# Odd mixing stage of a four-layer fp32 network: eight projection tiles multiplied by high and low rows in one product

## The reference, cut to what matters

```python
def odd_mixer(x, w_in, sgu_g, sgu_w, sgu_b, conv_w, w_o):
    h = x @ w_in
    u, v, g_b, g_c, z = _split(h, ODD_WIDTHS)          # five times 512 columns
    u = jax.nn.gelu(u)
    v = layer_norm(jax.nn.gelu(v).reshape(bsz, seq, G_C, HEAD_DIM), sgu_g)
    v = v.reshape(bsz, seq // CHUNK, CHUNK, G_C, HEAD_DIM)
    mix = jnp.einsum('gts,bnsgd->bntgd', jnp.tril(sgu_w), v) + jnp.swapaxes(sgu_b, 0, 1)[:, :, None]
    o_c = u * mix.reshape(bsz, seq, C_WIDTH)
    o_d = g_b * causal_dwconv(g_c * z, conv_w)
    return jnp.concatenate([o_c, o_d], axis=-1) @ w_o
```

## Time and profile before

| | us |
|---|---|
| median of 3 runs | 1352.31 (1351.74 to 1355.9) |
| the profiled execution's own time | 1356.57 |
| span of the profiled execution | 1355.3 |
| TensorE busy with matmuls in it | 1332.7 (98%) |
| VectorE (DVE) | 1011.4 (75%) |
| ScalarE (ACT) | 787.8 (58%) |
| GpSimd (POOL) | 147.2 (11%) |
| mean granted TensorE clock | 0.997 of full speed |

### The profile page before, as it was taken

How to read it: one execution, slowest core, us unless ns; L and a number is a source line. 1 busy time by engine, 2 the same in 40 slices (tenths; PEclk the granted TensorE clock), 3 DMA queues, 4 the chain that set the end, 5 groups by cost and what they waited for, 6 DMA issues and landing times. The chain is left out here.

```text
span 1355.3 us, 20736 instructions
## 1 busy us (share of the span) xinstructions
PE 1332.7 (98%) x8197; PEld 1160.7 (86%) x8197; DVE 1011.4 (75%) x1658; ACT 787.8 (58%) x1282; POOL 147.2 (11%) x131
## 2 busy tenths in 40 slices
PE   7999999999999999999999999999999999999998
PEld 7987888888898788887987888888789998888887
DVE  4845588777896787778788677776567997786766
ACT  6654266655442565653677566555557875665553
POOL 4860300000100000000000000000302224000000
PEclk9999999999999999999999999999999999999999
DMA  7722355655563556553642255655344345455551
GB/s 283 267 82 121 109 202 217 234 186 186 195 249 124 187 188 246 193 194 111 216 166 102 113 202 205 221 192 196 138 163 179 127 155 188 154 188 204 195 196 71
DMA packets 38607, 242.18 MB, mean 179 GB/s; under 512 B 4448, under 2 KB 7408, under 8 KB 11120
## 3 DMA queue, kind: packets, MB, share of 16 engines
q1 hardware_dynamic: 38512, 240.87, 48.6%
HBM read 236.89 MB, written 2.64 MB: 177 GB/s over the span
## 5 line engine op out<-in xcount | busy, mean ns | idle before, releaser
L323 DVE TENSOR_TENSOR wlo<-raw,whi 128x2048 fp32r<-128x2048 f32 (+1 forms) x179 | 402.6, 2255 | 105.1 <-ACT whi L297 103.1
L297 ACT ACTIVATE whi<-raw 128x2048 fp32r<-128x2048 f32 x195 | 370.4, 1903 | 88.8 <-PE ps L475 40.4
L412 PE MATMUL ps<-XS,whi 128*128 128x512 f32 x1392 | 331.8, 390 | 0.0
L412 PEld LDWEIGHTS ps<-XS,whi 128*128 128x128 f32 x1392 | 257.8, 188 | 52.2 <-issue 0.6
L464 PE MATMUL ps<-whi,MS 128*128 128x512 f32 x960 | 233.3, 391 | 0.0
L464 PEld LDWEIGHTS ps<-whi,MS 128*128 128x128 f32 x960 | 177.5, 188 | 35.8 <-issue 0.4
L417 PEld LDWEIGHTS ps<-XS,wlo 128*128 128x128 f32 x1392 | 178.5, 191 | 6.8
L417 PE MATMUL ps<-XS,wlo 128*128 128x256 f32 x1392 | 180.6, 283 | 0.0
L392 PE MATMUL ps<-XS,whi 128*128 128x256 f32 x672 | 167.2, 289 | 0.0
L393 PE MATMUL ps<-XS,whi 128*128 128x256 f32 x672 | 163.9, 284 | 0.0
L308 POOL TENSOR_TENSOR wlo<-raw,whi 128x512 fp32r<-128x512 f32 x90 | 123.1, 1381 | 188.6 <-ACT whi L297 98.4
(11 more groups left out here) (337 smaller groups left out, 1539.5 us busy)
## 6 DMA issues: line engine op xcount, KB each, us to landing
raw<-in_up SPq DMA_DIRECT2D x88, 1024.0 KB, 4.8
raw<-in_down SPq DMA_DIRECT2D x44, 1024.0 KB, 4.9
raw<-in_hg_t SPq DMA_DIRECT2D x16, 1024.0 KB, 4.8
raw<-in_od_t SPq DMA_DIRECT2D x8, 1024.0 KB, 5.2
raw<-in_ev_a SPq DMA_DIRECT2D x6, 1024.0 KB, 10.5
raw<-in_wa_o SPq DMA_DIRECT2D x6, 1024.0 KB, 5.0
raw<-in_hg_o SPq DMA_DIRECT2D x6, 1024.0 KB, 4.9
raw<-in_ev_o SPq DMA_DIRECT2D x4, 1024.0 KB, 5.8
```

The lines of the kernel that those rows point to most:

```text
L297: ac.activation(parts_of(m)[0][:, 0:w], raw[m % NRAW][:, 0:w], ACT.Copy).then_inc(w_hi)
L323: ve.tensor_tensor(lo[:, c], r[:, c], hi[:, c].bitcast(F32), ALU.subtract).then_inc(w_lo_v)
L412: pe.matmul(banks[i][:, 0:512], hi[:, c], XS[:, k, 0:512], start=(k == 0), stop=False)
```

## The change

All eight `ot` tiles go through `project_wide` instead of `project`. So each takes two banks, and the halves are added behind it. For u: ACT copies two low halves to `U` (`u_half`), DVE adds (`u_sum`), and ACT applies gelu in place (`u_gate`). For g_c and z: ACT copies both (`GC`, and the new `GD`), DVE adds each and then multiplies. For g_b: ACT copies into `XT`, DVE adds and then multiplies. The banks are dealt out anew, TensorE waits for `o_ua` and `o_vg` where it waited for `o_u`, the waits for `o_x` before the last two tiles go, and a wait for `o_x` at 6 comes before the output product.

```diff
+        GD = [R(256), yb[:, 1, 520:776]]
+        XT = [GC[0], GC[1], GD[0], GD[1]]
+        UB, ZBANK = [[bank[4], bank[5]], [bank[6], bank[7]]], [[bank[2], bank[3]], [bank[0], bank[1]], [bank[4], bank[5]], [bank[6], bank[7]]]
+        XB = [[bank[1], bank[3]], [bank[5], bank[7]]]
+        MIX = [bank[2], bank[0], bank[4], bank[6]]
 
         def odd_pe():
...
-            project(ot, bank[4])
-            project(ot + 1, bank[5])
+            project_wide(ot, UB[0])
+            project_wide(ot + 1, UB[1])
             filled(1)
-            project(ot + 2, bank[6])
-            project(ot + 3, bank[7])
-            pe.wait_ge(o_u.sem, 1)
-            project(ot + 4, bank[4])
-            pe.wait_ge(o_u.sem, 2)
-            project(ot + 5, bank[5])
+            project_wide(ot + 2, ZBANK[0])
+            pe.wait_ge(o_vg.sem, 2)
+            project_wide(ot + 3, ZBANK[1])
+            pe.wait_ge(o_ua.sem, 1)
+            project_wide(ot + 4, ZBANK[2])
+            pe.wait_ge(o_ua.sem, 2)
+            project_wide(ot + 5, ZBANK[3])
...
             for j in range(2):
-                pe.wait_ge(o_x.sem, j + 1)
-                project(ot + 6 + j, bank[6 + j])
+                project_wide(ot + 6 + j, XB[j])
+            pe.wait_ge(o_x.sem, 6)
             output(oo, 8, ms_ready(M0))
 
         def odd_act():
...
-            for j in range(2):
-                act_weights(ot + j + 2)
+
+            def u_half(j):
                 ac.wait_ge(w_done, DONE[ot + j])
-                ac.activation(U[:, 512 * j:512 * j + 512], bank[4 + j][:, :], ACT.Gelu_apprx_tanh).then_inc(o_u.up())
+                for i in range(2):
+                    c = 512 * j + 256 * i
+                    ac.activation(U[:, c:c + 256], UB[j][i][:, 256:512], ACT.Copy).then_inc(o_uc.up())
+
+            def u_gate(j):
+                ac.wait_ge(o_ua.sem, j + 1)
+                c = slice(512 * j, 512 * j + 512)
+                ac.activation(U[:, c], U[:, c], ACT.Gelu_apprx_tanh).then_inc(o_u.up())
+
+            act_weights(ot + 2)
+            u_half(0)
+            act_weights(ot + 3)
             ac.wait_ge(o_sq.sem, 1)
             ac.activation(XC, VG, ACT.Square).then_inc(o_sx.up())
+            u_gate(0)
+            u_half(1)
             ac.wait_ge(o_sw.sem, 1)
             ac.activation(WH, SW, ACT.Copy).then_inc(o_wh.up())
+            u_gate(1)
             for i in range(4):
                 act_weights(ot + i + 4)
...
-                ac.activation(GC[i % 2], bank[[6, 7, 4, 5][i]][:, 0:256], ACT.Copy).then_inc(o_gc.up())
+                ac.activation(GC[i % 2], ZBANK[i][0][:, 256:512], ACT.Copy).then_inc(o_gc.up())
+                ac.activation(GD[i % 2], ZBANK[i][1][:, 256:512], ACT.Copy).then_inc(o_gc.up())
...
             for j in range(2):
                 act_weights(ot + 6 + j + 2)
+                ac.wait_ge(w_done, DONE[ot + 6 + j])
+                ac.wait_ge(o_z.sem, 4)
+                for i in range(2):
+                    ac.activation(XT[2 * j + i], XB[j][i][:, 256:512], ACT.Copy).then_inc(o_xc.up())
...
         def odd_dve():
...
             dve_weights(ot + 3)
+
+            def u_sum(j):
+                for i in range(2):
+                    ve.wait_ge(o_uc.sem, 2 * j + i + 1)
+                    c = slice(512 * j + 256 * i, 512 * j + 256 * i + 256)
+                    ins = ve.tensor_tensor(U[:, c], UB[j][i][:, 0:256], U[:, c], ALU.add)
+                ins.then_inc(o_ua.up())
+
+            u_sum(0)
             ve.wait_ge(o_sx.sem, 1)
             ve.tensor_reduce(S2, x3, AX.X, ALU.add).then_inc(dv.up())
...
+            u_sum(1)
             dve_weights(ot + 4)
...
-                ve.wait_ge(o_gc.sem, i + 1)
-                ve.tensor_tensor(zb[:, 2:258], GC[i % 2], o[:, 256:512], ALU.mult).then_inc(o_z.up())
+                ve.wait_ge(o_gc.sem, 2 * i + 1)
+                ve.tensor_tensor(a, ZBANK[i][0][:, 0:256], a, ALU.add).then_inc(dv.up())
+                ve.wait_ge(o_gc.sem, 2 * i + 2)
+                ve.tensor_tensor(b, ZBANK[i][1][:, 0:256], b, ALU.add).then_inc(dv.up())
+                ve.wait_ge(dv.sem, dv.n)
+                ve.tensor_tensor(zb[:, 2:258], a, b, ALU.mult).then_inc(o_z.up())
...
             for j in range(2):
-                ve.wait_ge(w_done, DONE[ot + 6 + j])
                 for i in range(2):
                     c = 2 * j + i
-                    ve.tensor_tensor(OX[c % 2], OY[c], bank[6 + j][:, 256 * i:256 * i + 256], ALU.mult).then_inc(o_x.up())
+                    ve.wait_ge(o_xc.sem, c + 1)
+                    ve.tensor_tensor(XT[c], XB[j][i][:, 0:256], XT[c], ALU.add).then_inc(dv.up())
+                    ve.wait_ge(dv.sem, dv.n)
+                    ve.tensor_tensor(OX[c % 2], OY[c], XT[c], ALU.mult).then_inc(o_x.up())
```

More of the change, by code:

```diff
@@ L1674, in program @@
         r_sg = mark("r_sg")
+        o_uc, o_ua, o_xc = mark("o_uc"), mark("o_ua"), mark("o_xc")
+        GD = [R(256), yb[:, 1, 520:776]]
[3 more added lines that the diff above has]
+        MIX = [bank[2], bank[0], bank[4], bank[6]]
         def odd_pe():
@@ L1690, in odd_pe @@
             for c in range(4):
-                o = bank[[6, 7, 4, 5][c]]
+                o = MIX[c]
                 pe.wait_ge(o_z.sem, c + 1)
@@ L1787, in odd_dve @@
                     ve.tensor_tensor(XL, XC, XH.bitcast(F32), ALU.subtract).then_inc(o_wl.up())
-                zb, y, o = ZB[i], OY[i], bank[[6, 7, 4, 5][i]]
+                zb, y, a, b = ZB[i], OY[i], GC[i % 2], GD[i % 2]
                 w = [col("oc", 3 * i + k) for k in range(3)]
-                ve.wait_ge(o_gc.sem, i + 1)
-                ve.tensor_tensor(zb[:, 2:258], GC[i % 2], o[:, 256:512], ALU.mult).then_inc(o_z.up())
+                ve.wait_ge(o_gc.sem, 2 * i + 1)
[4 more added lines that the diff above has]
+                ve.tensor_tensor(zb[:, 2:258], a, b, ALU.mult).then_inc(o_z.up())
                 ve.wait_ge(o_z.sem, i + 1)
@@ L1806, in odd_dve @@
                     ins = ve.tensor_tensor(v(OX[c % 2][p, :]), v(U[p, 256 * c:256 * c + 256]),
-                                           v(bank[[6, 7, 4, 5][c]][p, :])[:, :, 128 * r:128 * r + 128], ALU.mult)
+                                           v(MIX[c][p, :])[:, :, 128 * r:128 * r + 128], ALU.mult)
                 ins.then_inc(o_x.up())
```

## The result

The changed kernel takes 1363.91 us (median of 6 runs, 1361.25 to 1366.62); the kernel before, measured in the same comparison, 1355.73 us (6 runs, 1351.74 to 1356.31). The ratio is 1.0065, with a 95% interval of 1.0051 to 1.0078: 8.8 us slower (6.9 to 10.6). A second comparison, with other runs of both, gave 1.0069 (1.0056 to 1.0082). The forecast was +8.9 us (a ratio of 1.0066), to 1361.2 us, in a range of 1356.2 to 1364.2.

A forecast was written before the change was run, and what follows sets the result against it. TensorE was taken to bound the kernel (busy 1332.7 of 1355.3 us), with DVE's order setting the changed stage. DVE's lateness of 6.1 + 1.8 + about 1.0 gave +8.9 us on 1352.3: 1361.2 us, range 1356.2 to 1364.2.

The forecast's parts named there:

- The walk along DVE: DVE's instructions followed in written order from u's adds to the layer norm: 8.9 us late at the end.
- I take 0: Clock fall ahead of the feed-forward layer, where TensorE would idle some 2.5 us: cost taken as 0, bounds 0 and 1.6.
- The sum: All DVE lateness added up, +8.9 us, set on a base of 1352.3 us to give 1361.2.
- TensorE's saving: Wide products of the eight `ot` tiles: 5.57 us a tile instead of 5.76, 1.5 us in all, spent waiting.
- Step 1, u: At u's adds, DVE waits for ACT's high part of `ot+4` behind the gelu: 2.6 us, DVE 2.97 us late.
- Steps 2 to 4: g_c and z adds, mixing products, g_b: u times mix 6.1 us late, output product 5.9 us late.
- the 1.4 us that cost nothing: At the output product: TensorE is free 1.4 us before `o_x` reaches 6, so a clock fall up to that is free.
- step 5: Behind the output product's start: last splits, load of `in_up`, layer norm and feed-forward layer all 8.9 us late.
- rival (b): At the layer norm: the output product's end governs, not the split of `in_up`; +4.2 us, 1356.5; chance 0.17.
- rival (c): Main forecast plus a clock fall ahead of the feed-forward layer: +10.5 us, 1362.8; chance 0.15.
- (d): DVE's added work hides in its waits and TensorE's 1.5 us saving stands: 1350.8; chance 0.05, given jointly with (e).
- (e): The wide matmul saves nothing on TensorE, turning (d) into no change; chance 0.05, given jointly with (d).

The follow-up runs named there:

- e1: The changed kernel with ACT's split of `ot+4` written ahead of the gelu of u's second half; ratio to the kernel before 1.0057.
- e5: The kernel before with one wait added: ACT may split `ot+4` only after DVE's norm of v; ratio 1.0019.
- e2: The changed kernel with DVE's split of `in_up` moved behind the layer norm; ratio to the kernel before 1.0058.
- e3: The kernel before, narrow products kept, with DVE's split of `in_up` moved behind the layer norm; ratio 0.9997.
- e9: The changed kernel with ACT's split of `ot+4` ahead of the gelu and DVE's work reordered, `in_up` split behind the norm; ratio to the kernel before 0.9981.
- e12: The changed kernel measured again without any edit; ratio to the kernel before 1.0069.
- e8: The changed kernel with `ot+4` split before gelu, `in_up` split behind the norm, and low parts of `ot+4` to `ot+7` shared with GpSimd; ratio to before 1.0053.
- e10: The kernel before, narrow products kept, with the new order of DVE's work; ratio 0.9987.
- e4: The changed kernel with both ACT's split of `ot+4` ahead of the gelu and DVE's split of `in_up` behind the norm; ratio to the kernel before 1.0023.
- e6: The changed kernel with u's two tiles put back to narrow products, the other six wide; ratio to the kernel before 1.0039.
- e11: The changed kernel with DVE's new order, but ACT's split of `ot+4` still behind the gelu; ratio to the kernel before 0.9996.

## Where the prediction held, and the steps that failed

The walk along DVE held to a few tenths of a microsecond. The step that failed is the choice "I take 0" for a fall of the clock ahead of the feed-forward layer: it fell in both traces of the changed kernel and cost 1.7 and 1.5 us, so the layer's second tile came 9.7 and 10.7 us late instead of 8.9. The sum was also set on a base that was too low, 1352.3 us, the median of three runs; with six it is 1355.73. That is 3.4 us, more than the 2.7 us by which the measured 1363.91 exceeds the 1361.2 of the forecast. That the ratio's 8.8 us stands so near the 8.9 is in part luck: from the first `ot` matmul to the end the two traces of the changed kernel are 9.6 and 10.5 us longer than that of the kernel before.

**TensorE's saving.** Right: 5.57 us a tile, and 1.56 us in all once nothing hides it. The 2.5 ns a pair of the Trainium skill (TensorE: Matmul & The Clock Gate, Back-to-back issue gap) would have made it 0.3 us, an estimate; these traces, where each matmul loads its own weights, don't bear that out: 1.56 us for 128 merged pairs is 12 ns a pair.

**Step 1, u.** Right: DVE was to wait from 385.8 to 388.35, and waited, less the 0.40 of the stage's start, up to 388.26. e1 takes the wait away and gets its 2.60 us; e5 makes it in the kernel before.

**Steps 2 to 4.** The size of DVE's lateness was right (u times mix 6.05 against 6.1). TensorE's waits were 3.67 and 1.23 us, forecast as 3.9 and 1.6. What was mis-sized is the fall of the clock there: it cost 0.74 us in the fourth mixing product (410.36 - 408.68 = 1.68 against 0.94) and 1.51 in `ot+6`, 2.25 together and not 1.6, so it used up the 1.4 us that cost nothing. `o_x` stood at 6 when it was forecast to (L1857 ends at 422.27, less 0.40 that is 421.9), but TensorE was free only at 423.01: the output product started 6.6 us late instead of 5.9. As the prediction said, the rest stayed off the path of step 5.

**Step 5.** The last splits: 8.8 us late against the 8.9 forecast. The wait of `in_up` in front of the norm was as read, and e2 shows it: with the split behind the norm, the norm's second half of rows starts 4.2 us later than before (77.9 against 73.7), the figure of rival (b), but not by its road, and its outcome didn't follow. (b) reckoned with an output product 5.9 us late and its end; in e2 it is 6.8 late, and the second half of rows simply follows the first by 5.78 us (5.72 before). The second tile is then 5.6 us late and the ratio stands at 7.9 us, not at 4.2, since TensorE's own work from the output product to the layer (30.0 us, in e2, e3 and e9 alike, without idle time) is what binds. The term that was off is the 7.98 us from the issue of `in_up` to its split on DVE: 7.17 here, 8.38 in e12, so the norm was 8.0 late in one trace and 9.2 in the other.

**The clock ahead of the feed-forward layer.** This is the choice that was wrong. I took 0 and gave the fall a chance of 0.15. It fell in both traces of the changed kernel, behind a wait of TensorE of 2.18 and 2.68 us, and in the first it cost 0.98 us in the products ahead of the layer (L636: 456.69 - 454.32 = 2.37 us, against 447.36 - 445.97 = 1.39 before) and 0.73 in the first tile: 1.7 us. So what happened was rival (c). In the first trace the norm came 0.9 us earlier than I had it, so 8.0 + 1.7 = 9.7 us at the second feed-forward tile, where I had 8.9; in e12 it came 0.3 later, 9.2 + 1.5 = 10.7.

**Rivals (d) and (e).** (d) fell at the point named: the product for i = 3 came at a distance of 42.3 where TensorE wanted it at 36.2. e9 shows that it is reachable by order alone. (e) fell with the tiles' 5.57 us.

What stays open: no run has the adds for g_c and z alone, so their share of the 9.7 us is the walk's (3.1) and not measured. And why the granted clock falls near 1170 us in the executions of e2, e8 and e10 and not in the others. It lies far behind the change.

## What to carry to other kernels

Before work is moved from an engine that is always busy to one that has spare time on the average, walk through the second engine's instructions in their written order: here 3.2 us of spare in a stretch of 38.5 met 4.9 us of adds and a wait of 2.5, and 1.5 us gained on TensorE became 9 lost. An instruction that waits for a result of the change must not be written ahead of one that other engines already wait for (the gelu ahead of the split), and a prefetch must not be written ahead of work on the critical path, since here its load is issued by that same engine's progress, so that a delay ahead of it holds up both. And TensorE, made to wait, may pay twice, since its clock can fall.

## What the hardware showed that I had not expected

TensorE's granted clock fell to 1.2 GHz behind waits of only 0.66 and 1.09 us (e5), shorter than the 2.25 us of the earlier trace rows; a fall cost 1.5 to 2.3 us of matmul time in the traces where it was read off. The waits alone don't decide it: e1 and e4 have the same two waits in the mixing products, 1.79 and 1.45 us, and behind them the granted clock was 1.00 in e1 and 0.62 (from 405 to 408 us) in e4; behind a single wait there, of 1.47 us in e6 and 1.26 in e11, it stayed 1.00. GpSimd's subtractions in SBUF made DVE's SBUF-only instructions that began beside them 1.7 to 3.6 times as long (0.42 to 0.73 us at L1832, 1.22 to 2.29, 0.35 to 1.27), and left those with an operand in PSUM as they were (e8).
